# A two-layer decoder trunk: the first loads in 256 KB pieces on two queues, fewer warming products, one conversion moved

## The reference

```python
for i in range(DEPTH):
    j = i // 2
    if i % 2 == 0:
        m = dsa_stick_mixer(h, even_w_in[j], even_kv_norm[j], even_w_uk[j], even_w_uv[j], even_w_out[j])
    else:
        m = moba_mixer(h, odd_w_in[j], odd_w_out[j])
    h = layer_norm(DEEPNORM_ALPHA * h + m, ln_mix_g[i], ln_mix_b[i])
    f = swiglu(h, ffn_gate[i], ffn_up[i], ffn_down[i])
    h = layer_norm(DEEPNORM_ALPHA * h + f, ln_ffn_g[i], ln_ffn_b[i])
```

## Time and profile before

| | |
|---|---|
| median of 3 runs | 598.82 us (598.73 to 599.18) |
| the profiled execution's own time | 598.94 us |
| its span, first to last instruction | 597.2 us |
| TensorE products busy | 589.1 us, 99% |
| VectorE busy | 424.4 us, 71% |
| ScalarE busy | 342.3 us, 57% |
| GpSimd busy | 26.6 us, 4% |
| moved by DMA | 109.43 MB, mean 183 GB/s |

### The profile page before, as it was taken

One profiled execution on the slowest core, in us unless ns is written; L12 is line 12 of the kernel. 1 busy time (PEld: TensorE's weight loads), 2 busy tenths in 40 slices (PEclk: granted clock), 3 DMA queues, 4 the chain that ended last, 5 costly groups with the idle time before them and its releaser, 6 DMA issues.

```text
span 597.2 us, 9595 instructions
## 1 busy us (share of the span) xinstructions
PE 589.1 (99%) x3354; PEld 505.7 (85%) x3354; DVE 424.4 (71%) x697; ACT 342.3 (57%) x645; POOL 26.6 (4%) x49
## 2 busy tenths in 40 slices
PE   8999999999999999999999999999999999999995
PEld 7988888888888888888888888888888888888885
DVE  4699877876776556655887888768677666665637
ACT  5776986456655544554556767645565555555530
POOL 1111111100000000000010000002000000000000
PEclk9999999999999999999999999999999999999999
DMA  8755437286676565564447543662767655555401
GB/s 309 265 179 194 142 124 245 91 291 202 223 223 207 193 205 181 182 205 140 143 148 270 180 141 117 205 207 80 237 217 234 210 202 165 185 186 189 140 1 70
DMA packets 30112, 109.43 MB, mean 183 GB/s; under 512 B 3376, under 2 KB 3376, under 8 KB 29952
## 3 DMA queue, kind: packets, MB, share of 16 engines
q1 hardware_dynamic: 28368, 102.25, 51.9%
q0 software_dynamic: 1568, 6.23, 3.4%
q10 hardware_dynamic: 144, 0.52, 0.2%
HBM read 107.94 MB, written 1.05 MB: 183 GB/s over the span
## 4 chain that ended last, share of the span: by engine, by line
PE 98%; DMA 1%; DVE 0%; DVEq 0%; issue 0%; ACT 0%; ACTq 0%
PE bank L1244 27%; PE bank L1152 24%; PE bank L1158 13%; PE bank L1694 5%; PE bank L1522 3%; PE bank L1698 3%; PE bank L1145 2%; PE bank L1222 2%; PE bank L1197 2%; PE bank L1198 2%; PE bank L1204 2%; PE bank L1339 1%; PE bank L1350 1%; PE bank L1330 1%; PE bank L1526 1%; PE bank L1501 1%
## 5 line engine op out<-in xcount | busy, mean ns | idle before, releaser
L753 DVE TENSOR_TENSOR wboth<-raw,wboth 128x1024 fp32r<-128x1024 f32 x190 | 225.3, 1223 | 44.5 <-ACT wboth L376 43.6
L376 ACT CAST wboth<-raw 128x1024 fp32r<-128x1024 f32 x190 | 191.2, 1047 | 21.6 <-DMA raw<-stream_in 20.8
L1152 PE MATMUL bank<-hTs,wboth 128*128 128x512 f32 x640 | 152.2, 390 | 0.0
L1244 PE MATMUL bank<-wboth,oThi 128*128 128x512 f32 x468 | 150.1, 392 | 0.0
L1152 PEld LDWEIGHTS bank<-hTs,wboth 128*128 128x128 f32 x640 | 118.8, 188 | 23.7
L1244 PEld LDWEIGHTS bank<-wboth,oThi 128*128 128x128 f32 x468 | 88.0, 188 | 18.3 <-issue 0.7
L1244 PE MATMUL bank<-wboth,oTlo 128*128 128x512 f32 x234 | 91.3, 390 | 0.0
L1158 PEld LDWEIGHTS bank<-hTs,wboth 128*128 128x128 f32 x640 | 81.9, 191 | 3.0
L1158 PE MATMUL bank<-hTs,wboth 128*128 128x256 f32 x640 | 83.2, 283 | 0.0
L1244 PEld LDWEIGHTS bank<-wboth,oTlo 128*128 128x128 f32 x234 | 44.0, 188 | 8.1
L654 ACT COPY kT<-bank 128x256 f32<-128x256 f32 x40 | 14.8, 371 | 58.8 <-PE bank L1158 58.7
(11 more groups left out here) (189 smaller groups left out, 635.1 us busy)
## 6 DMA issues: line engine op xcount, KB each, us to landing
raw<-stream_in SPq DMA_DIRECT2D x190, 512.0 KB, 4.9
qT<-ln_rows_in POOLq DMA_DIRECT2D x8, 512.0 KB, 5.1
kT<-stream_in SPq DMA_DIRECT2D x2, 512.0 KB, 6.2
h<-x_in POOLq DMA_DIRECT2D x1, 1024.0 KB, 5.0
out<-h SPq DMA_DIRECT2D x4, 256.0 KB, 2.1
v<-xT_in ACTq DMA_DIRECT2D x1, 512.0 KB, 5.1
v<-xT_in SPq DMA_DIRECT2D x1, 512.0 KB, 6.6
dist<-consts_in POOLq DMA_DIRECT2D x1, 384.0 KB, 3.5
```

The source lines that it names most:

```text
L376: nc.scalar.copy(whi[:, c % RING, j * HW:(j + 1) * HW], raw[:, c % RAW, j * HW:(j + 1) * HW]).then_inc(whi_ready, 1)
L753: nc.vector.tensor_tensor(wlo[:, c % RING, cols], raw[:, c % RAW, cols], whi[:, c % RING, cols].bitcast(F32), ALU.subtract).then_inc(wlo_r ...
L1152: mm(dst[:], whi[:, slot, off + k * P:off + (k + 1) * P], hTs[:, k].rearrange("p j s -> p (j s)"), start=(k == 0), stop=False)
L1244: last = mm(bank[4 + 2 * t + a][:], o[:, kts[j], t * P:(t + 1) * P], w[:, c % RING, j * D + a * 512:j * D + (a + 1) * 512], start=(start a ...
```

## The change

Six transfers of 256 KB and one of 512 KB take the place of four of 512 KB; SyncE issues four of them and ScalarE three. `xT` gets a semaphore for each pair of slices and chunk 0 gets three. TensorE waits before k = 0, 2, 4, 6 for the pair of slices, and before k = 0 and 4 for the quarter of the weights that these four use. The warming products are seven instead of ten. ScalarE converts the second half of chunk 2 ahead of the wait for `chunk_used` and the four copies instead of behind them.

```diff
-            sp.dma_start(first[:, FIRST[0]], stream[0][:, FIRST[0]]).then_inc(first_loaded[0], 16)
-            sp.dma_start(hT[:, 4:8], xT[:, 4:8]).then_inc(xT_loaded[1], 16)
-            sp.dma_start(first[:, FIRST[1]], stream[0][:, FIRST[1]]).then_inc(first_loaded[1], 16)
+            sp.dma_start(first[:, QUARTER[0]], stream[0][:, QUARTER[0]]).then_inc(first_loaded[0], 16)
+            for b in (1, 2):
+                sp.dma_start(hT[:, 2 * b:2 * b + 2], xT[:, 2 * b:2 * b + 2]).then_inc(xT_loaded[b], 16)
+            sp.dma_start(first[:, CW // 2:], stream[0][:, CW // 2:]).then_inc(first_loaded[2], 16)
...
-        WARM = 10
+        WARM = 7
...
-            act.dma_start(hT[:, 0:4], xT[:, 0:4]).then_inc(xT_loaded[0], 16)
+            act.dma_start(hT[:, 0:2], xT[:, 0:2]).then_inc(xT_loaded[0], 16)
+            act.dma_start(first[:, QUARTER[1]], stream[0][:, QUARTER[1]]).then_inc(first_loaded[1], 16)
+            act.dma_start(hT[:, 6:8], xT[:, 6:8]).then_inc(xT_loaded[3], 16)
             act.preload_act_table_set("natural_log_exp_and_others")
             def first_quarter(i):
-                act.wait_ge(first_loaded[i // 2], 16)
+                act.wait_ge(first_loaded[2], 16)
                 nc.scalar.copy(whi[:, 0, QUARTER[i]], first[:, QUARTER[i]]).then_inc(first_hi, 1)
 
             for b in range(4):
-                act.wait_ge(xT_loaded[b // 2], 16)
+                act.wait_ge(xT_loaded[b], 16)
                 nc.scalar.copy(hThi[:, 2 * b:2 * b + 2], hT[:, 2 * b:2 * b + 2]).then_inc(hThi_ready, 1)
             first_quarter(2)
             first_quarter(3)
             split_hi(1)
             split_hi_half(2, 0)
+            split_hi_half(2, 1)
             act.wait_ge(chunk_used, 1)
...
             nc.scalar.copy(kiT[DH:P], bank[4][0:DH, 0:S]).then_inc(proj_evac, 1)
-            split_hi_half(2, 1)
             split_hi_half(3, 0)
...
-            pe.wait_ge(first_loaded[0], 16)
             for k in range(KT):
                 if k % 4 == 0:
-                    pe.wait_ge(xT_loaded[k // 4], 16)
+                    pe.wait_ge(first_loaded[k // 4], 16)
+                if k % 2 == 0:
+                    pe.wait_ge(xT_loaded[k // 2], 16)
                 mm(bank[4][:, 0:S], first[:, k * P:(k + 1) * P], hT[:, k, :], start=(k == 0), stop=(k == KT - 1))
```

More of the change, by code:

```diff
@@ L111, in build @@
         first = kT[:].rearrange("p k s -> p (k s)")
-        FIRST = [slice(i * CW // 2, (i + 1) * CW // 2) for i in range(2)]
         QUARTER = [slice(i * CW // 4, (i + 1) * CW // 4) for i in range(4)]
@@ L132, in build @@
         raw_loaded = [[sem(f"raw_loaded{i}{j}") for j in range(2)] for i in range(RAW)]
-        xT_loaded = [sem(f"xT_loaded{i}") for i in range(2)]
-        first_loaded = [sem(f"first_loaded{i}") for i in range(2)]
+        xT_loaded = [sem(f"xT_loaded{i}") for i in range(4)]
+        first_loaded = [sem(f"first_loaded{i}") for i in range(3)]
         first_hi, first_lo = sem("first_hi"), sem("first_lo")
```

## The result

The changed kernel takes 599.84 us (599.63 to 600.09), the kernel before 598.84 (598.49 to 599.28), 22 runs of each: 1.00 us slower, ratio 1.0016 with a 95% interval of 1.0010 to 1.0022. The forecast was 598.5 in a range of 597.8 to 599.2. The profiled execution of the changed kernel took 599.63, its span is 597.9. That is the shortest of its 22, so the two traces are 0.69 us apart where the medians are 1.00 apart; the other 0.3 is scatter between executions that no trace shows.

What follows compares the result with a forecast made beforehand. The prediction took DMA arrival of the first 2 MiB, ahead of L1387, as the bound; -0.3 (loads) + 0 (warming) + 0 (conversion) gave 598.64 for the profiled execution, 598.5 for the median, range 597.8 to 599.2.

Steps and rivals of the forecast that it cites:

- What bounds the kernel: At the start, arrival of the first 2 MiB by DMA decides when L1387 starts (9.96), not the first product.
- the carry-over: After L1387, the difference of the two times equals the difference of the two L1387 starts; nothing later has its own clock.
- L1387 after 10.2: Sign of being wrong: L1387 starting after 10.2 us, where 9.3 to 9.9 was forecast.
- part 1: First loads as 256 KB pieces on two queues, used pair by pair: -0.3 us, between -0.63 and +0.2.
- +0.2 end: First loads: 2 KB rows may move 5% slower on 1.5 MB, losing 0.2 us.
- -0.63 end: First loads: if the slow rate of 5 to 8 us goes, 258 KB come sooner, gaining 0.63 us.
- (b): First loads: a tax per piece from 2 KB rows and three more issues, 599.0 to 600.1, likeliest 599.2; chance 0.11.
- (c): L1375: TensorE stays at or falls back to 1.2 GHz, ending 1.5 us later, kernel 600.3; chance 0.04.
- Part 2: Start of TensorE: seven warming products for ten free it in time for the first pair; 0 at the end of L1375.
- (e): L1375: waits only rearranged, pair one landing with pair two at 5.8; 598.8, chance 0.26 shared with the nothing-gained rival.
- 6 us: First loads: the skill's fit, with its fixed part paid in line, puts three further copies at an estimated 6 us.
- Part 3: Chunk 2: converting its second half ahead of four copies changes 0 now, raising TensorE's time in hand from 0.9 to 1.9.

Runs made afterwards that it cites:

- e9: Kernel before with chunks 1 and 2 loaded in eight transfers of 256 KB instead of four of 512 KB: 598.90 us, ratio 0.9995.
- e10: Kernel before with the four 512 KB transfers of chunks 1 and 2 taking two runs of 2 KB per partition: 600.39 us.
- e7: Kernel before with two SyncE issues swapped, the second half of chunk 0 ahead of activations 4 to 7: 600.34 us.
- e1: Changed kernel with ten warming products and the old place of the conversion again, so only loads and their waits changed: 599.67 us, ratio 1.0014.
- e8: Kernel before with its four first 512 KB transfers each taking two runs of 2 KB per partition instead of one of 4 KB: 601.92 us.
- e2: Kernel before with seven warming products and the conversion of chunk 2 moved ahead of the four copies, loads as before: 599.82 us.
- e6: Kernel before with only the warming products cut from ten to seven: 599.64 us.
- e14: Changed kernel with each 256 KB piece contiguous in device memory, rows 2 KB apart instead of 8 KB: 599.02 us, ratio to before 0.9998.
- e5: Kernel before with only the conversion of chunk 2 moved ahead of the four copies: 598.86 us, ratio 1.0001.
- e15: Kernel before with its four first 512 KB transfers each contiguous in device memory, rows 4 KB apart instead of 8 KB: 598.33 us, ratio 0.9990.
- e13: Changed kernel with one 512 KB half of chunk 1 issued on each queue ahead of the small pieces: 603.08 us.
- e3: Changed kernel with all seven first transfers issued by SyncE, in a slightly different order: 602.80 us.
- e4: Changed kernel with each 256 KB piece cut as 64 partitions with 4 KB rows instead of 128 with 2 KB rows: 602.86 us.
- e11: Kernel before with its four first 512 KB transfers each taking four runs of 1 KB per partition: 604.79 us.

## Why the prediction was wrong

**What bounds the kernel** held. The landing of 2 MiB and not the first product as the question, and the early start given back as a wait inside L1375 are what the trace after shows; of the two things that end at L1387 the conversion of the last piece now came last, 0.24 us after the products. So did the carry-over: 0.84 at L1387 is 0.78 at the end. Of the signs set down for being wrong, L1387 after 10.2 is the one that came, at 10.80.

**The step that failed is the rate in part 1**, the term of -0.3 between the ends -0.63 and +0.2. It measured +0.87 at the last landing. Both ends came from the wrong rows. The +0.2 end was taken from GpSimd's queue at 20 to 22 us, read as rows of 2 KB. The row does not show that: 96 packets with 0.31 MB are 3.2 KB each, while ScalarE's pieces in the changed kernel came in 432 packets with 0.79 MB, 1.8 KB each. That e9 and e10 then measured nearly this price (1.33 for 1.28) behind a full queue is luck. And the pieces of the change stand in the first 8 us, where the whole loss was four times as high. The -0.63 end supposed that the slow stretch was SyncE alone on the activations. e7 put weights there and it stayed (225 GB/s in 6 to 7 us), e1 had both queues at work and it stayed (195). So what ran in the place of the gain was a loss: the pairs forecast for 7.2 to 7.9 landed at 8.4 and 9.3, the last piece, forecast for 8.5 to 9.2, at 10.0. The earlier trace rows had shown 59 and 324 GB/s in stretches where nothing but the first loads runs, and I treated slowness at the start as something that could only improve.

**The rivals.** (b), a tax per piece, was the case that came: 599.0 to 600.1 with likeliest 599.2, at a chance of 0.11, against 599.84 measured. Its size was inside; of its two reasons, three more issues are not needed, as e8 lands as late with four transfers, and 2 KB rows cost 4% where e9 and e10 measured them, not what was lost here. (c), the clock, did not show in the trace of the changed kernel, but e2 and e6 show that it was no idle fear: the same seven products with the old loads cost 0.8 to 2.0 us in about half of the executions. Part 2 at 0 held with the new loads, for the reason given, that "the waits that follow hide it": in e14's trace they do. It holds only together with part 1, which the prediction did not say. Its reading of the lower level compared products of two shapes (0.44 for 512 columns, 0.216 for 256) and comes out right all the same, since L1152's, of 512 columns as well, are 0.23 apart later on (16 in 3.65 us). (e) did not come: pair one landed at 5.0, 0.4 later than taken, and pair two at 6.0 to 6.2. The fit that the prediction takes from the Trainium skill stands in "DMA: Bandwidth & Descriptors", section "Anatomy of one DMA — SWDGE (gpsimd) path", for copies that GpSimd issues. The seven here are issued by SyncE and ScalarE, so its 6 us were no estimate for them.

**Part 3** was right: 0 (e5).

**The chances.** The verdict "within 0.2%" holds (1.0016), but the way was the wrong one, and the range did not hold, since its upper end took in only the lower part of (b).

**Cause, as far as it is shown.** The four or seven first transfers read rows of 4 or 2 KB at a pitch of 8 KB in device memory. That the loads make the loss is shown (e1, with e5 and e6 for the other two parts), and so is where: the last piece lands 0.87 later because the first 8 us move fewer bytes. Why they do is in part argued. Packed, the 4 KB rows are faster: e15 differs from the kernel before only in this layout and the tensor added for it, and lands 1.1 us sooner; e14 against the changed kernel comes out 0.8 lower in the median, but its one trace does not show the pieces landing sooner. Shorter rows in the unpacked form go with a later landing (e8, and the change), at the very start much more than behind 1 MiB of larger transfers, by the estimate from e13. What stays open is why the pitch matters for so short a time: the chunks that follow have the same 8 KB pitch and run at 410 to 420 GB/s from 9 us on, and in e15 it is the first of them, at 8 to 9 us, that is slow. That fits "the first transfers at this pitch are slow" better than "the first 8 us are slow", but no run separates the two, nor the pitch from the place of the new tensor; 1 KB rows at 381 GB/s in 3 to 5 us do not fit a simple rule of rows either.

## What to carry to other kernels

Take the price of a load from the same moment of the kernel: a rate measured behind a full queue says little of the first microseconds, where the same pieces lost several times as much. Try laying out what is loaded first as contiguous blocks before cutting it into pieces, and look at the transfers that follow, where the slow stretch may turn up again. Do not shorten the warming of TensorE on the word of one profile: look at the spacing of the products and at the spread of many runs, since one profile may show only the good kind. When an experiment reorders loads, look for other transfers that are issued on their landings, as GpSimd's was in e13.

## What the runs showed of the hardware

- Pieces of 256 KB on one queue at the start (e3) landed at 4.1, 5.3, 6.0 and then not before 10.1: 174 GB/s in 5 to 8 us with the DMA engines 0.81 busy. The same seven on two queues, in a slightly different order, ended 3.0 us sooner, of which the earlier issue is 1.4. The Trainium skill, "DMA: Bandwidth & Descriptors", section "Issuing engines are not separate DMA queues", says that issuing from several engines saves only the time of issuing; here it saved 1.6 us more.
- Transfers over 64 partitions took the DMA engines 1.7 times as long per byte: 238 GB/s at a share of 1.01 (e4, 5 to 8 us), against 410 at the same share over 128 partitions.
- With the first loads at the 8 KB pitch 6 to 7 us is slow (254 before, 180 after, 225 in e7 and e9), with activations or with weights under way; with short rows the dip lies elsewhere or is flatter (277 and 289 in 6 to 8 us in e8, 261 in 5 to 6 in e11). Packed in halves (e15), 6 to 7 us runs at 414 and the dip comes at 8 to 9, at 201, with the first unpacked transfer. The same page's section "Latency and other measured facts" tells of lower rates at row pitches of large powers of two, from 512 KiB up, and gives padding or contiguous tiles as the cure; the runs here show lower rates at 8 KB, for the first transfers only, and do not show that the pitch is the cause.
- With seven warming products and 1.2 to 1.3 us idle behind them about half of the executions are 0.8 to 2.0 us longer (e2, e6), and the one traced (e2) has products 0.45 us apart. Idle time is not needed for it: e14 has none and slow products up to 6.7. Nor is it enough: e6's trace has 1.18 us idle and none. Ten products do not exclude it, as e8 shows (0.82 us idle, slow until 10.4); with 0.6 us idle 89 of 96 runs are below 599.4. After 4.4 us idle (e11) the granted clock was 0.50.
